# The opening of a two-layer diffusion trunk: x asked for first, small parameter rows on ScalarE's queue and behind, three projection tiles opened together

## The reference, cut to what matters

```python
def trunk_layer(x, cond, ctx_k, ctx_v, p):
    sh1, sc1, gt1, sh2, sc2, gt2 = modulation(cond, p['w_mod'], p['b_mod'])   # silu(cond) @ w_mod + b_mod
    h = rms_norm(x, p['norm1_g']) * (1.0 + sc1) + sh1
    q, k, v, u = mixer_projections(h, p['w_in'], ...)                         # h @ w_in, then q and k normed
    attn = block_attention(q, keys, vals)                                     # rotary q, k; cached context keys
    pooled = pool_mixer(u, p['w_pool'], p['pool_scale'])
    x = x + gt1 * (concatenate([attn, pooled], -1) @ p['w_out'])
    h2 = rms_norm(x, p['norm2_g']) * (1.0 + sc2) + sh2
    return x + gt2 * conv_ffn(h2, p['w_up'], p['conv_w'], p['conv_b'], p['w_down'])
```

## Time and profile before

| | us |
|---|---|
| median of 3 runs | 1442.25 (1441.65 to 1442.99) |
| span of the profiled execution, first to last instruction | 1439.4 |
| PE busy | 1407.3 (98%) |
| DVE busy | 903.1 (63%) |
| ACT busy | 534.1 (37%) |
| POOL busy | 400.5 (28%) |

### The profile page before, as it was taken

The page is one execution under the profiler, slowest core; times in us unless marked ns, Lnnn a source line. Parts: engine busy times, 40 slices in busy tenths (PEclk is TensorE's granted clock), DMA queues, the critical chain, the costliest instruction groups (busy, mean ns, idle before and its releaser), DMA issues.

```text
span 1439.4 us, 25053 instructions
## 1 busy us (share of the span) xinstructions
PE 1407.3 (98%) x9905; PEld 1353.2 (94%) x9905; DVE 903.1 (63%) x1429; ACT 534.1 (37%) x798; POOL 400.5 (28%) x273
## 2 busy tenths in 40 slices
PE   6999999999999999999999999999999999999997
PEld 4888889999999999999999977999999999999997
DVE  4448869897966478785775787369744323444333
ACT  5436862533231123232242587344233112232322
POOL 0264002153440033433205800214433101323321
PEclk9999999999999999999999999999999999999999
DMA  9752005253535334335423200224323312222321
GB/s 315 248 178 80 1 2 161 81 166 106 164 121 162 94 117 145 120 120 153 120 58 86 63 1 2 59 89 132 104 79 90 87 57 67 73 73 73 101 61 74
DMA packets 198158, 147.05 MB, mean 102 GB/s; under 512 B 4400, under 2 KB 187448, under 8 KB 197048
## 3 DMA queue, kind: packets, MB, share of 16 engines
q1 hardware_dynamic: 196592, 144.27, 32.8%
q10 hardware_dynamic: 1480, 1.57, 0.3%
HBM read 142.94 MB, written 2.88 MB: 101 GB/s over the span
## 4 chain that ended last, share of the span: by engine, by line
PE 87%; DVE 7%; ACT 2%; issue 2%; SPq 1%; DMA 1%; DVEq 0%; ACTq 0%
PE pair L1468 68%; PE pair L1484 7%; PE pair L1865 3%; PE pair L1910 3%; PE pair L1879 2%; DVE mod_acc L1050 1%; DVE in_lo L1116 1%; DVE norm_t L1106 1%; SPq L414 1%; DVE conv L1390 1%; DMA w_first<-in_w_mod_dram 1%; DVE w_lo L1027 1%; DVE small L1328 1%; PE pair L1768 1%; PE pair L1720 1%
## 5 line engine op out<-in xcount | busy, mean ns | idle before, releaser
L1468 PE MATMUL pair<-in_hi,w_hi 128*128 128x384 f32 x1728 | 396.1, 310 | 0.2
L1468 PE MATMUL pair<-in_lo,w_hi 128*128 128x384 f32 x1728 | 394.7, 309 | 0.0
L1468 PE MATMUL pair<-in_hi,w_lo 128*128 128x384 f32 x1728 | 392.7, 308 | 0.0
L1390 DVE SCALAR_TENSOR_TENSOR conv<-pair,vec,conv 128x127 f32<-128x127 f32 x352 | 168.7, 541 | 193.4 <-ACT conv L935 192.9
L1468 PEld LDWEIGHTS pair<-in_hi,w_hi 128*128 128x128 f32 x1728 | 265.4, 189 | 5.6 <-issue 2.2
L1468 PEld LDWEIGHTS pair<-in_lo,w_hi 128*128 128x128 f32 x1728 | 265.6, 189 | 0.0
L1468 PEld LDWEIGHTS pair<-in_hi,w_lo 128*128 128x128 f32 x1728 | 263.6, 188 | 0.0
L636 POOL TENSOR_TENSOR silu_a<-silu_a,conv 128x640 f32<-128x640 f32 x44 | 113.0, 2567 | 534.2 <-DVE conv L1390 534.2
L935 ACT ACTIVATE conv<-pair,vec 128x640 f32<-128x640 f32 x88 | 77.8, 886 | 407.5 <-PE pair L1468 405.3
L1027 DVE TENSOR_TENSOR w_lo<-w_raw,w_hi 128x1024 fp32r<-128x1024 f32 (+1 forms) x148 | 195.7, 1322 | 38.4 <-ACT w_hi L658 37.9
L658 ACT ACTIVATE w_hi<-w_raw 128x1024 fp32r<-128x1024 f32 (+1 forms) x82 | 96.9, 1182 | 287.1 <-PE pair L1468 270.5
(11 more groups left out here) (205 smaller groups left out, 1775.5 us busy)
## 6 DMA issues: line engine op xcount, KB each, us to landing
w_raw<-in_w_up_dram SPq DMA_DIRECT2D x88, 512.0 KB, 3.8
mod_raw<-in_w_mod_dram SPq DMA_DIRECT2D x64, 512.0 KB, 4.4
w_raw<-in_w_down_dram SPq DMA_DIRECT2D x32, 704.0 KB, 4.6
w_raw<-in_w_in_dram SPq DMA_DIRECT2D x20, 512.0 KB, 4.2
w_first<-in_w_mod_dram SPq DMA_DIRECT2D x16, 512.0 KB, 8.8
w_raw<-in_w_out_dram SPq DMA_DIRECT2D x16, 512.0 KB, 4.1
mod_raw<-in_w_mod_dram SPq DMA_DIRECT2D x4, 1024.0 KB, 5.1
mod_acc<-in_w_mod_dram SPq DMA_DIRECT2D x4, 1024.0 KB, 5.0
```

The source lines that it names most:

```text
L1390: ins = dve.scalar_tensor_tensor(out=conv[:, s, d0:d1], in0=up_result(g, j, s)[:, d0 + sh:d1 + sh], scalar=v(L, V_TAP[t], s * NF + g * FG ...
L1468: ins = pe.matmul(dst[:, a:e], w[:, s, k, :], rhs[:, kk, a:e], start=first and r == 0, stop=last and r == 2)
```

## The change

The opening is rearranged; the arithmetic stays the same.

- SP asks for x first. The identity and the condition rows go to ACT's queue, ahead of its parameter rows; the taps and the final gain move from ACT's queue to SP's, behind the first two projection tiles. `fold`, the edges and the rotation tables are separate tensors now and come later.
- x is turned through three PSUM places; ACT empties rounds 3, 5 and 7, DVE the others. Filler matmuls (identity by identity) stand ahead of the first round (4) and between its tiles (2 each), and 12 ahead of the first product. The first half of modulation block 0 and two of the six row tiles go between the rounds, the other four row tiles behind the first block's products.
- ACT copies the spread 1/rms to SBUF. Tile 1's high part is made by POOL, its low part by DVE behind `in_lo` of block 0. Tile 2 has its own places (`third_hi`, `third_lo`, `third_raw`).
- PE runs blocks 0 and 1 for tiles 0 and 1, then the same blocks for tile 2, then blocks 2 to 7 for all three tiles.

```diff
+        def xt_place(k):
+            return (pair[0], pair[1], pair[3])[k % 3]
...
-            for i, src in enumerate((c_ctx, c.rearrange("a d -> (a d)"))):
-                sp.dma_start(cond_rows[i * NK:(i + 1) * NK, :], src.rearrange("(r c) -> r c", c=P)).then_inc(s_crow, 16)
-            sp.dma_start(ident, consts[:, 0:P]).then_inc(s_const0, 16)
-            sp.dma_start(fold, consts[:, n_const - P:n_const]).then_inc(s_const0, 16)
...
+            load_first(1)
+            sp.wait_ge(s_xsq, 4)
+            sp.dma_start(third_raw, w_in_v[0][:, :, IN_COLUMN[2]:IN_COLUMN[2] + P]).then_inc(s_third, 16)
...
+            sp.wait_ge(s_lin, 3)
+            sp.dma_start(turn[:, :], consts[:, 3 * P:3 * P + 2 * TS]).then_inc(s_turn, 16)
...
+            pool.wait_ge(s_raw[1], 16)
+            pool.wait_ge(s_whi, 1)
+            pool.tensor_copy(w_hi[:, 1, 0:NK, :], w_raw[:, 1, 0:NK, :]).then_inc(s_whi, 1)
...
+            act_e.wait_ge(s_bc, 1)
+            act_e.activation(spread_x, lin[3], ACT.Copy).then_inc(s_spread, 1)
+            first_copied(0)
             hi(0, 0, NK)
             for k in range(NK):
...
                 act_e.activation(in_hi[:, k, :], sq[:, k % 2, :], ACT.Copy).then_inc(s_hhi, 2)
+                if k == 0:
+                    vec_copied(VEC_REST, 3)
+                if k % 2 == 1 and k + 1 < NK:
+                    first_copied((k + 1) // 2)
+                if k == 1:
+                    hi_own(2)
...
             for k in range(NK):
+                dve.wait_ge(s_hhi, 2 * (k + 1))
+                dve.tensor_tensor(in_lo[:, k, :], sq[:, k % 2, :], in_hi[:, k, :].bitcast(F32), ALU.subtract).then_inc(s_h, 2)
+                if k == 0:
+                    lo(1, 1, NK)
                 if k + 2 < NK:
                     scaled_x(k + 2)
                 if k % 2 == 1 and k + 1 < NK:
                     first_mod((k + 1) // 2)
+                if k == 1:
+                    lo(2, 0, NK)
...
+            keep_busy(4, pair[3][:, 512:512 + P])
             for k in range(NK):
...
+                    if k == 0 and b < NT - 1:
+                        keep_busy(2, pair[3][:, 512:512 + P])
                 ins.then_inc(s_xt, 1)
+                if k == 5:
+                    first_sums(0, 0)
+                    pe.wait_ge(s_rows, 16 * (5 + 4))
+                    vec_turned(VEC_FIRST)
...
+            first_sums(0, 1)
             first_columns(0)
+            for k in (6, 7):
+                x_emptied(k)
+            keep_busy(12, pair[0][:, 0:P])
...
+                    opened_hi(0, (0, 1))
+                    opened_lo(0, (0, 1))
+                    pe.wait_ge(s_rows_late, 16 * (3 + DEPTH))
+                    pe.wait_ge(s_vec, 1)
+                    vec_turned(VEC_REST)
+                    first_sums(1, 0)
+                    first_sums(1, 1)
+                    opened_hi(1, (0, 1))
+                    first_columns(1)
+                    opened_lo(1, (0, 1))
...
+                    for k in range(2):
+                        opened_hi(k, (2,))
+                        opened_lo(k, (2,))
+                    first_sums(2, 0)
...
+                    opened_hi(3, (0, 1, 2))
+                    first_columns(2)
+                    opened_lo(3, (0, 1, 2))
+                    first_sums(3, 0)
+                    opened_hi(4, (0, 1, 2))
...
+                    opened_hi(5, (0, 1, 2))
+                    first_columns(3)
+                    opened_lo(5, (0, 1, 2))
+                    for k in range(6, NK):
+                        opened_hi(k, (0, 1, 2))
+                        opened_lo(k, (0, 1, 2))
```

More of the change, by code:

```diff
@@ L150, in build @@
         n_const = consts.shape[1]
-        cst = sb("cst", [P, n_const])
+        cst = sb("cst", [P, 3 * P])
+        with ExitStack() as own:
+            third_hi = sb("third_hi", [P, NK, P], F32R, at=own)
+        turn = sb("turn", [P, 2 * TS])
+        n_edge = n_const - 4 * P - 2 * TS
+        tail = sb("tail", [P, n_edge + P])
         ident, head_ones, ones = (cst[:, i * P:(i + 1) * P] for i in range(3))
-        cos, sin = (cst[:, 3 * P + i * TS:3 * P + (i + 1) * TS] for i in range(2))
-        fold = cst[:, n_const - P:n_const]
-        edge = cst[:, 3 * P + 2 * TS:n_const - P].rearrange("p (g s e c) -> p g s e c", g=NPOOL, s=2, e=2)
+        cos, sin = (turn[:, i * TS:(i + 1) * TS] for i in range(2))
+        fold = tail[:, n_edge:n_edge + P]
+        edge = tail[:, 0:n_edge].rearrange("p (g s e c) -> p g s e c", g=NPOOL, s=2, e=2)
         vec = sb("vec", [P, DEPTH, 3, P])
@@ L160, in build @@
         eps = sb("eps", [P, 2])
+        with ExitStack() as own:
+            third_lo = sb("third_lo", [P, NK, P], F32R, at=own)
         wp = sb("wp", [P, NPOOL, P])
@@ L1189, in _ @@
                 dve.wait_ge(s_xt, k + 1)
[L1190 to L1191 removed]
+                dve.tensor_copy(x[:, k, :], xt_place(k)[:, 0:T]).then_inc(s_xe_dve, 1)
+                if k == XE_VECTOR[2]:
                     dve.wait_ge(s_sd, 1)
@@ L1214, in first_mod @@
                        .then_inc(*((s_fmod, 1) if m < NK - 1 else (s_gain, 1)))
-            dve.wait_ge(s_bc, 1)
-            for k in range(2):
-                scaled_x(k)
-            lo(0, 0, NK)
+            dve.wait_ge(s_spread, 1)
+            scaled_x(0)
             dve.wait_ge(s_vec, 1)
@@ L1790, in _, with opened_hi @@
-                    linear_pair(tile_in(L), NK, in_hi, in_lo, *h_wait(2 * L), first_ahead, first_between)
-                    linear_third(tile_in(L) + 2, NK, in_hi, in_lo, lin[2])
+                    opening = [(lin[s], w_hi[:, s, :, :], w_lo[:, s, :, :]) for s in range(2)] + [(lin[2], third_hi, third_lo)]
+                    def opened_hi(k, tiles):
+                        pe.wait_ge(s_hhi, 2 * (k + 1))
+                        for t in tiles:
+                            if k == 0:
+                                pe.wait_ge(s_wlo, t + 1)
+                            dst, w, l = opening[t]
+                            product(dst, w[:, k, :], in_hi[:, k, :], k == 0, False)
+                            product(dst, l[:, k, :], in_hi[:, k, :], False, False)
@@ new lines, in opened_lo @@
+                    def opened_lo(k, tiles):
+                        pe.wait_ge(s_h, 2 * (k + 1))
+                        for t in tiles:
+                            dst, w, _ = opening[t]
+                            ins = product(dst, w[:, k, :], in_lo[:, k, :], False, k == NK - 1)
+                            if k == NK - 1:
+                                ins.then_inc(s_lin, 1)
+                    opened_hi(0, (0, 1))
+                    opened_lo(0, (0, 1))
+                    pe.wait_ge(s_rows_late, 16 * (3 + DEPTH))
```

172 lines of the change are left out of this document (79 added, 93 removed).

## The result

The change made the kernel slower: 1452.43 us (median of 5 runs, 1451.23 to 1454.13) against 1441.65 for the kernel before in the same session, a ratio of 1.0078 with a 95% interval of 1.0066 to 1.009. The forecast was 1447.4 with a range to 1451.0: the sign is right, the size is not.

What follows compares the result with a forecast made beforehand. PE, busy in 98% of the 1439.4 us span, was taken as the bound; -5.65 + 2.65 + 8.4 - 0.8 + 0.5 = +5.1 on 1442.25 gave 1447.4 us, range 1443.5 to 1451.0.

Steps and rivals of the forecast that it cites:

- tile 3 near 65: Sign of being right: the first projection's tile 3 starts near 65 us, against 59.93 before.
- a sign of being wrong: At the opening: among the signs listed, a tile 3 start that doesn't shift the end by as much.
- Terms 2 to 5: Behind the first product: moved work +2.65, new PE waits +8.4, old waits gone -0.8, tile 2's extra high-low turns +0.5.
- term 3: New PE waits at tile 1, block 1, tile 2, blocks 4 and 6, and tile 3: +8.4 us together.
- Term 1: Opening up to PE's first product: 5.65 us earlier, at 24.2 instead of 29.87; ends 23.6 and 25.8.
- PE may start its filler at 5.7: Start of the opening: ACT's table load ends at 5.45, then two Silu of some 0.1 each, then PE's fillers.
- is over before DVE needs it: Tile 1 at block 0: POOL's copy for the high part starts at 21 and doesn't delay DVE.
- against it, then, unless a wait grows: Argument against the clock falling in the new waits: PE's earlier wait of 1.94 was followed by products at usual pace.
- The rival in which the clock falls: Clock falls in PE's new waits; blocks 6 and 7 at half pace: +10.7, 1453.0 us; chance 0.06.
- A shift of tile 3's start is a shift of the end: Behind tile 3 of the first projection: order unchanged, later work waits for PE, so the sum is made there.
- Slower: Whole kernel: slower by over 0.2% (2.9 us), chance 0.80.

Runs made afterwards that it cites:

- after_again: The changed kernel itself, unaltered, measured once more: 1451.14 us against 1442.24 for the kernel before in that session.
- fill_late: The changed kernel with 7 fillers between the first late-modulation sums and tile 3: 1450.50 us.
- fill_all: The changed kernel with fillers in all of PE's waits of 0.9 us or more (first product, tile 2, blocks 4 and 6, tile 3): 1450.01 us.
- high_act: The changed kernel with tile 1's high part made by ACT behind the first normalised block, not by POOL: 1453.28 us.
- best1: Changed kernel, tile 2 alone behind tiles 0 and 1, taps' rows behind modulation weights, identity first on SP, tile 1's high part on ACT, further steps earlier: 1442.04 us.
- fill_both: The changed kernel with 16 fillers instead of 12 ahead of the first product, 4 between tiles 0 and 1 in block 0, 7 ahead of tile 3: 1450.16 us.
- ident_sp: The changed kernel with the identity first on SP's queue, ahead of x, and the condition rows first on ACT's: 1451.46 us.

## Why the prediction was wrong, step by step

The account below adds up the two traces of the changed kernel, in us against the kernel before. A fall is priced against a trace without one: the way from the first product to tile 3 takes 42.90 with the first fall and 40.66 without it (after_again), tile 3 takes 9.75 with the second and 8.20 without it (fill_late, fill_all).

| | first trace | after_again |
|---|---|---|
| forecast | 5.1 | 5.1 |
| first product later than 24.2 (25.61, 26.20) | 1.41 | 2.00 |
| from there to tile 3, 40.66 for the forecast's 40.83 | -0.17 | -0.17 |
| first fall of the clock | 2.24 | none |
| second fall of the clock | 1.55 | 1.55 |
| behind the start of tile 4 | 2.35 | 0.90 |
| span against 1439.4 | 12.5 | 9.4 |

So three steps failed. In the first trace the falls weigh most, in after_again the late first product. Of the prediction's own signs, tile 3 near 65 did not come (68.51 and 66.86), and a sign of being wrong did, in both traces: tile 3 shifted by 8.58 and 6.93, the end by 12.5 and 9.4.

**Terms 2 to 5 held.** From the first product (24.2) to tile 3 (59.93 + 5.1 = 65.03) the forecast gives 40.8. Where no fall lies between, the traces give 66.86 - 26.20 = 40.7 in after_again, 66.94 - 26.23 = 40.7 in fill_late and 66.88 - 26.13 = 40.8 in fill_all. The waits of term 3 in after_again are 1.18, 0.73, 1.69, 0.92, 1.92 and 2.04, together 8.5, against 8.4. That the sum fits so well is partly luck: five waits are 0.06 to 0.17 shorter than forecast, and tile 3's is longer, 2.04 for 1.5. Its low part took 1.83 and not 1.22, beside a sum on POOL; DVE, then POOL in the first trace:

```profile
66.53 1.83 DVE L1085 TENSOR_TENSOR w_lo<-w_raw,w_hi 128x1024 fp32r<-128x1024 f32 x1
```

```profile
65.99 1.29 POOL L636 TENSOR_TENSOR tree<-u 128x663 f32<-128x663 f32 x1 [10.93 <-DVE u L1356]
```

ACT stood still for 5.31 us behind its first block in the first trace, where some 4 were forecast; the fall lengthened it, and in after_again it was 4.29.

**Term 1 was mis-sized.** "The first product: 5.65 earlier" measured 4.26 in the first trace and 3.67 in after_again. x itself was there at about 11.3 in the first trace (last asked for at 2.6, 8.7 to its landing), near the 10.9 of the forecast. Two links failed. "PE may start its filler at 5.7": it started at 7.29, because the condition rows, now on ACT's queue beside x, landed at 6.59. The fillers then ran at the low pace for longer (eight rows in 2.04), and the last tile of x was turned at 12.30 and 13.12, not at 11.5. And POOL's copy, which "is over before DVE needs it", held DVE's first shift for 0.87 (high_act); the forecast had named that only as something nothing in the trace priced.

**The step that cost most in the first trace is a judgement, not a sum: "against it, then, unless a wait grows".** The rival in which the clock falls had a chance of 0.06, because before's wait of 1.94 brought no fall. One such wait in one trace says little. Over the traces of the three-tile kernels the count is: behind an open wait of 2.03 or 2.04 at tile 3 a fall in 5 of 5, behind one of 1.91 or 1.92 at block 6 in 1 of 8, behind tile 2's 1.69 in none of 8, behind the early waits, with tile 1's at 1.18 to 1.35, in 2 of 6, and none where these waits were filled. The Trainium skill, "TensorE: Matmul & The Clock Gate", "Why this matters for your kernels", warns of idle gaps between bursts; the traces agree that a gap can bring the half rate back, and show it behind shorter gaps than the page warns of. The length alone does not decide: waits of 1.94 brought no fall in the kernel before and in best1, and one of 1.92 did in fill_both. Why the same wait brings a fall in one execution and not in another was not tested beyond repeating it. The price had also been set for the wrong place: blocks 6 and 7 at half pace would have cost 5.6, while the two falls of the first trace cost 2.24 and 1.55. So it is luck that this rival's 1453.0 lies so near the measured 1452.43; the other two steps of the account are not in it.

**"A shift of tile 3's start is a shift of the end" did not hold either:** behind the start of tile 4 the first trace loses another 2.35 us. Of these, 1.3 arise at the start of the first MLP, where DVE and POOL work side by side. DVE before and after:

```profile
291.68 2.47 DVE L1050 SCALAR_TENSOR_TENSOR mod_acc<-mod_raw,cond,mod_acc 128x1024 f32<-128x1024 f32 x2
```

```profile
301.81 3.78 DVE L1108 SCALAR_TENSOR_TENSOR mod_acc<-mod_raw,cond,mod_acc 128x1024 f32<-128x1024 f32 x2
```

and POOL before and after:

```profile
291.84 3.73 POOL L636 TENSOR_TENSOR silu_a<-silu_a,conv 128x640 f32<-128x640 f32 x1 [21.77 <-DVE conv L1390]
```

```profile
301.97 2.53 POOL L683 TENSOR_TENSOR silu_a<-silu_a,conv 128x640 f32<-128x640 f32 x1 [21.77 <-DVE conv L1451]
```

The two engines start with the same distance, 0.16, and their times add up to 6.20 and 6.31; who of them waits has changed, and DVE stands on the chain to PE. In after_again it did not change and the 1.3 is missing, so this part belongs to the execution. The 13 traces of changed kernels bear this out: the four in which DVE took 3.78 lose 2.2 to 2.4 behind tile 4, the other nine 0.9 to 1.3.

The other 1.0 arises in layer 1, at the start of the attention: in each of the 13 traces the low part of one layer 1 tile takes 2.49 or 2.50 beside POOL's sums, where it took 1.23 before. DVE before and after:

```profile
783.40 1.23 DVE L1027 TENSOR_TENSOR w_lo<-w_raw,w_hi 128x1024 fp32r<-128x1024 f32 x1 [4.05 <-ACT w_hi L658]
```

```profile
794.85 2.49 DVE L1085 TENSOR_TENSOR w_lo<-w_raw,w_hi 128x1024 fp32r<-128x1024 f32 x1 [4.42 <-ACT w_hi L705]
```

This is also where best1 loses the 0.84 that it has gained at tile 4. There is one trace of the kernel before, so whether this part is the change's or chance stays open; that all 13 traces have it, and that best1's median is not below the kernel before's, speaks for the change.

**The chances.** "Slower" at 0.80 was right, and so were the place and the names of the waits. The range failed at its upper end, because it left out the one rival whose price lay above it and put what is behind tile 3 at nothing.

## What to carry to other kernels

A wait that a change adds is not paid by its length alone: where PE waits 1 to 2 us and then runs dense matmuls, add the price of a fall of the clock (here 1.55 and 2.24 us) with a real chance, and put the top of the range there. A product that starts earlier gains nothing if the transfer behind it keeps its landing: best1 began its products 6.2 us earlier and met the same half block at 28.14 instead of 28.87. A shift at the opening need not arrive at the end: where two engines work side by side further on, who of them waits can change, here for 0.9 to 2.4 us. And tiles that end together uncover the preparation of the next one, which a tile run alone had hidden.

## What the runs showed of the hardware

- The granted clock can fall behind a wait of about 2 us (5 of 5 at tile 3), and the same kernel with the same waits shows a fall in one execution and none in the next (28 us in the first trace and in after_again). Waits of 1.94 brought none in the kernel before and in best1. With fillers in the wait at tile 3 there was no fall in 3 of 3.
- A DVE operation of 128 by 2 elements took 1.10 instead of 0.23 while POOL copied a tile for 1.04. The Trainium skill, "SBUF — State Buffer", "Who interferes with whom", says that where a DVE instruction needs the ports that DVE shares with GpSimd, one of the two engines holds them for a whole instruction and the other stands still; the times above agree. Which of the two went next at the first MLP was different in executions with equal distances: in 4 of 14 traces it was POOL.
- Asking for x 1.2 to 1.7 us earlier moved the landing of the weights behind it by 0.15 to 0.73 us (28.87 before, 28.72, 28.44 and 28.14 in three orders of the requests).
- The identity and the condition rows on ACT's queue, beside x's large transfers, were all there at 6.59; on SP's queue ahead of x they had been there at 3.96. With the identity ahead of x on SP's queue and the rows first on ACT's it was 5.10 (ident_sp).
